# The hand-over from router and shared expert to the routed experts, the way expert rows leave PSUM, and the final sum, in a one-layer hybrid SSD, attention and MoE block

## The reference

```python
n2 = rms_norm(h, norm2_g) * (1.0 + sc2) + sh2
# moe_ffn: 64 experts of hidden width 256, top 6 for each token
scores = sigmoid(n @ router_w)          # choice of 4 of 8 groups, then of 6 experts
w = w / sum(w) * 2.5
out = (silu(n @ s_gate) * (n @ s_up)) @ s_down          # shared expert, all tokens
for e in range(64):
    hid = silu(n @ e_gate[e]) * (n @ e_up[e])
    out = out + (hid @ e_down[e]) * combine[:, e:e + 1]
h = h + g2 * out
return rms_norm(h, final_g)
```

## Time and profile before

| | |
|---|---|
| time, median of 3 runs | 1333.85 us (1332.2 to 1335.52) |
| profiled execution | 1334.45 us |
| its span, first to last instruction | 1332.7 us |
| PE busy | 1208.2 us, 91% |
| DVE, ACT, POOL busy | 455.9, 270.8, 199.2 us |
| mean granted TensorE clock | 0.965 |
| moved by DMA | 322.30 MB, 242 GB/s |

### The profile page before, as it was taken

How to read it: one execution, slowest core, us unless ns; L and a number is a source line. 1 busy time by engine, 2 the same in 40 slices (tenths; PEclk the granted TensorE clock), 3 DMA queues, 4 the chain that set the end, 5 groups by cost and what they waited for, 6 DMA issues and landing times.

```text
span 1332.7 us, 13517 instructions
## 1 busy us (share of the span) xinstructions
PE 1208.2 (91%) x4819; PEld 621.5 (47%) x4819; DVE 455.9 (34%) x985; ACT 270.8 (20%) x657; POOL 199.2 (15%) x321
## 2 busy tenths in 40 slices
PE   3999999998999999999998999999999899988855
PEld 1545865455554454458743444434443344433322
DVE  4567034656565101114743222212121212111116
ACT  2141121134341000001211222212121212111101
...
GB/s 301 176 96 93 64 127 95 69 58 127 158 130 281 87 134 32 95 113 291 128 103 224 329 333 416 422 424 421 420 411 396 420 397 404 368 421 419 228 266 197
DMA packets 107435, 322.30 MB, mean 242 GB/s; under 512 B 14340, under 2 KB 67672, under 8 KB 80872
## 3 DMA queue, kind: packets, MB, share of 16 engines
...
HBM read 314.49 MB, written 26.82 MB: 256 GB/s over the span
## 4 chain that ended last, share of the span: by engine, by line
PE 80%; DMA 6%; DVE 6%; issue 3%; SPq 3%; ACT 1%; POOL 0%; POOLq 0%; DVEq 0%; ACTq 0%
PE ps L1741 21%; PE ps L1589 13%; PE ps L1749 10%; PE ps L1372 7%; PE ps L1380 4%; DMA gu_lo<-in_exp_w_up_dram 4%; PE ps L1617 4%; PE ps L1408 3%; PE ps L1729 3%; PE ps L1562 2%; PE ps L1818 2%; PE ps L1670 2%; DVE seg L1011 1%; PE ps L1690 1%; SPq L392 1%
## 5 line engine op out<-in xcount | busy, mean ns | idle before, releaser
L1741 PE MATMUL ps<-gu_hi,xsT 128*64 128x512 f32 (+1 forms) x672 | 222.3, 624 | 23.4 <-DMA gu_hi<-in_exp_w_up_dram 12.8
L1741 PEld LDWEIGHTS ps<-gu_hi,xsT 128*64 128x64 f32 (+1 forms) x672 | 86.6, 167 | 137.9 <-issue 137.5
L1291 DVE SCALAR_TENSOR_TENSOR hid<-ps,wgt,gated 128x256 f32<-128x256 f32 x42 | 20.3, 484 | 339.5 <-ACT gated L877 339.5
L1589 PE MATMUL ps<-n1T,ring 128*128 128x512 f32 x256 | 112.5, 600 | 3.7 <-DVE mod L1117 3.0
L1741 PE MATMUL ps<-gu_lo,xsT 128*64 128x512 f32 (+1 forms) x352 | 95.4, 660 | 20.4 <-issue 16.1
L1372 PE MATMUL ps<-n1T,ring 128*128 128x512 f32 x256 | 111.9, 594 | 0.0
L1749 PE MATMUL ps<-dn_hi,hidT 128*64 128x512 f32 (+1 forms) x336 | 108.6, 596 | 0.0
L648 POOL DMA_INDIRECT expert_rows<-hn,meta x42 | 41.9, 997 | 421.0 <-DVE hn L1287 400.0
L877 ACT ACTIVATE gated<-ps 128x256 f32<-128x256 f32 x42 | 16.1, 384 | 331.8 <-PE ps L1741 331.8
L1589 PEld LDWEIGHTS ps<-n1T,ring 128*128 128x128 f32 x256 | 49.1, 193 | 65.3 <-issue 61.4
L1372 PEld LDWEIGHTS ps<-n1T,ring 128*128 128x128 f32 x256 | 48.1, 190 | 58.7 <-issue 58.7
...
## 6 DMA issues: line engine op xcount, KB each, us to landing
...
```

The costliest lines, as they stand in the source:

```text
L1589: ins = pe.matmul(ps[:, 4 * jj + b, :], w[:, k, P * jj:P * jj + P], src[:, k, :], start=(k == 0), stop=(k == KC - 1))
L1741: ins = pe.matmul(ps[rows, 2 + b, :], xsT[:, b, k, rows], gu(s)[:, :, k, :], start=(k == 0), stop=(k == KC - 1))
```

## The change

Five things change. (1) On PE all four `shared_gu` come ahead of the first `shared_down`, with results in banks 0, 1, 5, 6 (`SH_BANK`); `router(3)` is issued after two instead of four matmuls of `shared_gu(1)`, `positions(3)` before `shared_down(0)`, and the first `turn_in` before `shared_down(2)` instead of behind `shared_down(3)`. (2) POOL's wait for the second shared tile before its first gather is gone, since the shared results go through `ys` and no longer through all of `hn`; DVE fills the lists' upper halves (`upper`) before `add_shared(0)`. (3) SP loads slots 4 and 5 in two pieces: gate and up of both and down of slot 4 once all `shared_gu` are done and the first gather has landed, down of slot 5 once the last `shared_down` is done. (4) `rows_out`: DVE alone takes a unit's 128x1024 result from PSUM, times g2; ACT's `half_y` is gone, and g2 is no longer applied in the tail. (5) The tail's rows come in three DMAs of 1 MB for a tile, each with a semaphore of its own, and PE starts on the first; DVE adds its two rows and `h` before it waits for PE.

```diff
-            tile(own, "until_merged", [P, UNTIL_MERGED])
+            marks = tile(own, "marks", [P, UNTIL_MERGED])
...
+        SH_BANK = (0, 1, 5, 6)
...
+        def two_rows(t, part):
+
+            return flat(dn(t)) if part == 2 else gu(t)[:, part, :, :].rearrange("p k f -> p (k f)")
+
+        def rows_in_part(t, part):
+
+            return (x_in[t], 48 if t == 0 else 32) if part == 2 else (early_in[2 * t + part], 48)
...
-            sp.wait_ge(ordered, TABLE)
+            ids = [sp.value_load(order[0:1, rank_of(n):rank_of(n) + 1], min_val=0, max_val=NE - 1)
+                   for n in (FIXED, FIXED + 1)]
+            sp.wait_ge(sgu_ready, T)
+            sp.wait_ge(gathered[0], 16)
+            load_gu(FIXED, ids[0])
+            load_dn(FIXED, ids[0])
+            load_gu(FIXED + 1, ids[1])
             sp.wait_ge(sy_ready, T)
-            for n in range(FIXED, SEQ0):
+            load_dn(FIXED + 1, ids[1])
+            for n in range(SLOTS, SEQ0):
                 e = sp.value_load(order[0:1, rank_of(n):rank_of(n) + 1], min_val=0, max_val=NE - 1)
-                if n >= SLOTS:
-                    sp.wait_ge(gu_ready, unit_of(n - SLOTS) + 1)
+                sp.wait_ge(gu_ready, unit_of(n - SLOTS) + 1)
                 load_gu(n % SLOTS, e)
-                if n >= SLOTS:
-                    sp.wait_ge(ey_ready, unit_of(n - SLOTS) + 1)
+                sp.wait_ge(ey_ready, unit_of(n - SLOTS) + 1)
                 load_dn(n % SLOTS, e)
...
-                sp.dma_start(gu(t)[:, :, :, :].rearrange("p a k f -> p (a k f)"), rows_v[:, t, 0:4 * D]).then_inc(x_in[t], 16)
-                sp.dma_start(flat(dn(t)[:, :, :]), rows_v[:, t, 4 * D:]).then_inc(x_in[t], 16)
+                for part in range(3):
+                    sp.dma_start(two_rows(t, part), rows_v[:, t, 2 * D * part:2 * D * part + 2 * D]).then_inc(rows_in_part(t, part)[0], 16)
...
-            pool.wait_ge(sy_added, 2)
...
-            def half_y(b, ready):
-                act.wait_ge(ey_ready, ready)
-                act.activation(ys[:, b, 0:BANK], ps[:, 5, :], ACT.Copy).then_inc(ey_act, 1)
...
+            shared_gate(1)
+            shared_gate(2)
+            shared_hT(0)
+            shared_gate(3)
+            shared_y(0)
+            shared_hT(1)
+            shared_y(1)
             turn_in(0, 1)
+            for t in (2, 3):
+                shared_hT(t)
+                shared_y(t)
...
-            add_shared(0)
...
+            def rows_out(b, ready):
+                dve.wait_ge(ey_ready, ready)
+                dve.tensor_tensor(ys[:, b, :], flat(ps[:, 5:7, :]), g2_row[:, :], ALU.mult).then_inc(ey_dve, 1)
...
+            shared_hid(1)
             shared_hid(2)
+            dve.wait_ge(lists_in, 32)
+            for un in range(3):
+                upper(un, NE + un)
+            add_shared(0)
...
+            turn_in(0, 1)
+            shared_hid(3)
             add_shared(1)
-            shared_hid(3)
...
-                dve.wait_ge(x_in[t], (64 if t == 0 else 48))
+                dve.wait_ge(*rows_in_part(t, 2))
                 chain(dve.tensor_tensor(total, total, dn(t)[:, 1, :], ALU.add))
+                chain(dve.tensor_tensor(h[:, t, :], h[:, t, :], total, ALU.add))
                 dve.wait_ge(tail_sum, t + 1)
-                chain(dve.tensor_tensor(total, total, flat(ps[:, 2 * t:2 * t + 2, :]), ALU.add))
-                chain(dve.tensor_tensor(total, total, g2_row[:, :], ALU.mult))
-                dve.tensor_tensor(h[:, t, :], h[:, t, :], total, ALU.add).then_inc(fsq_in, 1)
+                dve.tensor_tensor(h[:, t, :], h[:, t, :], flat(ps[:, 2 * t:2 * t + 2, :]), ALU.add).then_inc(fsq_in, 1)
...
+                if t == 2:
+                    pe.wait_ge(n2_dve, T)
+                if t == 3:
+                    pe.wait_ge(ordered, T)
...
-            shared_gu(1, range(KC // 2))
+            shared_gu(1, range(2))
             router(T - 1)
-            shared_gu(1, range(KC // 2, KC))
-            shared_down(0)
+            shared_gu(1, range(2, KC))
+            shared_gu(2, range(1))
             positions(T - 1)
             pe.wait_ge(score_done, T)
             for i, tokens_in in enumerate((three_tiles, sel[:, T - 1, :])):
                 ins = pe.matmul(ps[:, 7, 0:NE], ones[:, :], tokens_in, start=(i == 0), stop=(i == 1))
             ins.then_inc(rows_counted, 1)
-            shared_gu(2)
+            shared_gu(2, range(1, KC))
             pe.wait_ge(routed, PLACE)
             pe.matmul(ps[0:1, 7, NE:2 * NE], ecol[:, 0:1], place, start=True, stop=True).then_inc(counted, 1)
-            shared_down(1)
+            shared_gu(3)
...
-            shared_gu(3)
+            shared_down(0)
+            shared_down(1)
+            pe.wait_ge(shid_done, 2)
+            turn_in(0, 16)
             shared_down(2)
...
-                pe.wait_ge(x_in[t], (64 if t == 0 else 48))
-                rows = gu(t)[:, :, :, :].rearrange("p a k f -> p (a k f)")
-                for half in range(2):
-                    for k in range(4):
-                        ins = pe.matmul(ps[:, 2 * t + half, :], ident[:, :],
-                                        rows[:, D * k + BANK * half:D * k + BANK * half + BANK], start=(k == 0), stop=(k == 3))
+                for part in range(2):
+                    pe.wait_ge(*rows_in_part(t, part))
+                    for k in range(2):
+                        for half in range(2):
+                            ins = pe.matmul(ps[:, 2 * t + half, :], ident[:, :],
+                                            two_rows(t, part)[:, D * k + BANK * half:D * k + BANK * half + BANK],
+                                            start=(part == 0 and k == 0), stop=(part == 1 and k == 1))
...
```

More of the change, by code:

```diff
@@ L1272, in upper @@
                 dve.tensor_copy(wgt[HALF:P, c:c + 1], entry(1, col)[:, 1:2]).then_inc(upper_done, 1)
-            dve.wait_ge(lists_in, 32)
-            for un in range(3):
-                upper(un, NE + un)
             def turn_in(b, ready):
```

142 lines of the change are left out of this document (58 added, 84 removed).

## The result

| | before | after |
|---|---|---|
| median of the runs made together | 1335.52 us (1332.2 to 1336.23, 5 runs) | 1325.23 us (1323.47 to 1328.12, 5 runs) |
| ratio, 95% interval | | 0.9935 [0.9919, 0.9952] |
| profiled execution, its span | 1334.45, 1332.7 us | 1323.47, 1321.8 us |
| PE, DVE, ACT busy | 1208.2, 455.9, 270.8 us | 1203.9, 471.5, 250.6 us |

The change makes the kernel 0.65% faster, some 9 us. Two further sets of the changed kernel, made beside other experiments, gave 1324.66 (ratio 0.9934) and 1324.28 (0.9922). Forecast were 1322.6, with a range of 1319 to 1327.5. Against the median of 1333.85 that the forecast started from, it counted on a gain of 11.3 us; measured are 8.7 by the ratio and 10.3 by the two medians.

What follows compares the result with a forecast made beforehand. Limits: hand-over a chain over PE; units PE, then DMA; tail a chain. Span 1332.7 - 4.3 (hand-over) - 6.9 (tail) = 1321.5; with 1.75 around the span 1323.2, less 0.6 to the median: 1322.6 us, range 1319 to 1327.5.

Steps and rivals of the forecast that it cites:

- The walk: Hand-over: new order counted with old durations; PE's idle pieces sum to 6.1 against 7.68, first unit 1.5 us sooner.
- I take it that the fall doesn't come: Hand-over: PE's clock stays up, so the first `gate_up` takes 7.05 instead of 9.82, a gain of 2.8 us.
- rival (a): Hand-over: the clock still falls, two idle pieces lying close together; costs 1.7 to 2.8, time 1324.3 to 1325.4; chance 0.25.
- the case that the forecast held likeliest: Whole kernel: gains in both hand-over and tail, no fall of the clock, 1322.6 us; chance 0.5.
- the piece of 2.86: Hand-over before the change: PE idle 2.86 us until the first tokens are modulated; longest piece to fall to 1.1.
- Rival (c): Units: earlier loads count in full, 11 us passing through to the end, time 1316; chance 0.05.
- One sign: DMA queues: idle after the loads of slots 4 and 5 until PE's first slot is free at 720.
- Eviction: Units: one DVE instruction of 1.22, 0.54 later to the scatter, hidden except in the last unit, where it adds 0.5.
- Tail: Tail: PE starts 4.4 us sooner and 2.5 less follows its sums, 6.9 together; bounds 2.5 and 8.
- part 12: Tail: last DMA part of rows lands at 1312.1; DVE's two adds end at 1314.6, PE's sums at 1314.8.
- (d): Tail: PE stays at 1.2 GHz because each part is waited for apart, time 1347.4; chance 0.03.
- the estimate from rows: Tail: first 1.05 MB land 5.2 us after SP issues, 2.5 of moving plus 2.7 fixed.

Runs made afterwards that it cites:

- e9: The changed kernel with the first `turn_in` and its modulation back behind the last `shared_down`, all else as changed: 1323.4 us, ratio 0.9913.
- e8: The changed kernel with the last tile's two rows for DVE in two DMAs of 0.5 MB instead of one of 1 MB: 1324.83 us, ratio 0.9919.
- e2: The changed kernel with the tail's rows read back in two DMAs a tile, as before the change: 1327.97 us, ratio 0.9953.
- c1_all: The changed kernel with tile 2's transposes before the first `turn_in`, the last shared result in banks 5 and 6, DVE's last rows in two DMAs: 1319.47 us, ratio 0.9886.
- e3: The kernel before the change with only the new eviction and the new tail, hand-over as before: 1328.31 us, ratio 0.9953.
- e1: The changed kernel with all three loads of slots 4 and 5 put behind the end of the last `shared_down`: 1325.69 us, ratio 0.9934.
- e6: The changed kernel with the eviction as before, by ACT and DVE, and g2 applied in the tail: 1325.81 us, ratio 0.9944.
- a0_again: The changed kernel run once more without edit: 1324.66 us, ratio 0.9934.
- a0_third: The changed kernel run once more without edit, in another group: 1324.28 us, ratio 0.9922.

## Why the prediction was right, and what in it was not

**Hand-over, idle time: right.** The walk gave pieces that sum to 6.1; the trace has 0.37, 0.47, 1.22, 0.81, 1.63, 0.47 and 1.17, 6.14 in all. The gather was forecast at 695.4 and came at 695.16, its tokens at 699.6 and came at 699.29, the loads of the slots at about 700 and came at 699.38.

**Hand-over, clock: right about the first `gate_up`, wrong about the stage.** The step "I take it that the fall doesn't come" failed: it moved. The first `gate_up` took 7.13, but tile 2 took 5.40 behind the two idle pieces 0.81 and 1.63 that rival (a) named. That costs 1.7, the lower price of (a), and puts the time at 1324.3; the three sets gave 1325.23, 1324.66 and 1324.28. So the case that the forecast held likeliest came in only two profiles of nine. The gain of the stage is 2.4 with the fall and 4.0 without it, not 4.3.

**What made that gain: in part wrong.** The walk let the piece of 2.86 vanish because `turn_in` had moved. By e9 the earlier lists and the shared gate-up ahead of all downs suffice for the gain: the gather has then landed, and the wait for the modulated tokens is 1.90 instead of 2.86. Which of the two does it was not tested apart. In the middle of the list `turn_in` splits ACT's work and makes the piece of 1.63.

**Units: right.** The first wait for weights moved from 893.49 to 891.03, and from the second `gate_up` to the last it took 528.7 to 529.6 in twelve of fourteen profiles (e8 529.95, e2 530.52), while the second `gate_up` began anywhere from 718.85 (c1_all) to 728.00 (e3). What PE wins ahead of them comes out at their end; e1 shows that filling slots sooner does not. Rival (c) is out. One sign failed: the queues were to be idle from the end of the slots' loads until 720. They were at 0.97 to 1.11 from 702 to 720, and moved only 254 to 289 GB/s in 704 to 712. It cost nothing: in e1 the same loads came later still.

**Eviction: right.** One DVE instruction of 1.22, 0.50 later to SP, in the last unit alone (e6).

**Tail: right in sum, 6.5 against 6.9, but its last step ends elsewhere.** PE's start: 5.04 sooner after SP, less 0.50, is 4.5 against 4.4. Behind PE the prediction wanted 2.5 less, with part 12 "just in time" at 32.7 after SP. It came after 33.44, and DVE's two additions of it ended 1.16 behind PE: from the end of PE's sums to the end of DVE's last addition it took 3.85 before (to 1323.04) and 2.41 after, 1.44 less. PE's own sums were 0.6 shorter and made up part of it. In a0_again and a0_third they were 0.5 and 0.3 longer than before, the same piece took 1.45, and the end came no later: 37.19 and 37.10 after SP, against 37.18. So DVE's rows set the end and not PE's sums. Where PE does end last, in e2, the piece is 1.33, and the shorter chain gives its 2.5. (d) did not happen: no gap over 0.3 between the parts in after.

By an estimate from the Trainium skill's figures (DMA: Bandwidth & Descriptors, Anatomy of one DMA), which are fitted there to DMAs that GpSimd issues, the first part would have landed after 4.4. SP issues these, and PE's first sum began 5.13 after SP's DMA, so the estimate from rows, 5.2, was the better one.

**The sum.** The profiled span came out as forecast, 1321.8 against 1321.5, partly by luck: 1.9 less in the hand-over and 0.4 less in the tail than forecast were made up by 1.4 in the last `gate_up` and 0.4 at the start. The median lies 1.8 above that profiled execution, and 2.6 above the forecast.
